# Up projection of an MLP: GpSimd instead of VectorE forms four sums of each unit's rectified blocks

## What is computed

```python
x = x + mixed @ w_out[l]
h = _rms_norm(x, norm_mlp_g[l])
x = x + jnp.square(jax.nn.relu(h @ w_up[l])) @ w_down[l]
return _rms_norm(x, norm_final_g)
```

## Time and profile before

| | before |
|---|---|
| median of 3 runs | 1518.6 us |
| the profiled execution | 1519.8 us |
| its span in the profile | 1518.0 us |
| TensorE busy in the span | 98% |
| VectorE busy | 72% |
| ScalarE busy | 52% |
| GpSimd busy | 1%, 28 instructions |
| mean granted TensorE clock | 0.996 |

### The profile page before, as it was taken

The page is one execution under the profiler, slowest core; times in us unless marked ns, Lnnn a source line. Parts: engine busy times, 40 slices in busy tenths (PEclk is TensorE's granted clock), DMA queues, the critical chain, the costliest instruction groups (busy, mean ns, idle before and its releaser), DMA issues.

```text
span 1518.0 us, 20760 instructions
## 1 busy us (share of the span) xinstructions
PE 1492.6 (98%) x7307; PEld 1239.0 (82%) x7307; DVE 1088.4 (72%) x1743; ACT 792.8 (52%) x1439; POOL 16.2 (1%) x28
## 2 busy tenths in 40 slices
PE   7999999999999999999999999999999899999998
PEld 6888888887888888888888888888888678888887
DVE  5787777756686778543765686667667798888886
ACT  6577766665677775444234553333334444444442
POOL 0000000000000200000000000000000000000000
PEclk9999999999999999999999999999999999999999
DMA  5221111114222014334545434444445864444402
GB/s 194 71 70 29 43 56 43 29 45 98 74 70 71 15 43 125 98 104 148 182 134 141 139 98 164 155 153 152 153 153 166 300 240 153 152 153 153 153 28 111
DMA packets 171061, 176.78 MB, mean 116 GB/s; under 512 B 9576, under 2 KB 129736, under 8 KB 170576
## 3 DMA queue, kind: packets, MB, share of 16 engines
q1 hardware_dynamic: 170960, 175.46, 36.4%
HBM read 129.08 MB, written 46.35 MB: 116 GB/s over the span
## 4 chain that ended last, share of the span: by engine, by line
PE 89%; DVE 5%; ACT 2%; issue 2%; DMA 1%; SPq 0%; DVEq 0%; ACTq 0%
PE ps L1547 39%; PE ps L1206 20%; PE ps L1407 8%; PE ps L1151 4%; PE ps L1438 4%; PE ps L1282 3%; PE ps L1249 3%; PE ps L1261 3%; PE ps L1348 1%; PE ps L1175 1%; PE ps L1140 1%; DVE keep L2410 1%; DVE keep L2305 1%; DVE ps L2283 1%; PE ps L1295 0%
## 5 line engine op out<-in xcount | busy, mean ns | idle before, releaser
L1206 PE MATMUL ps<-hspl,wsp 128*128 128x512 f32 x1536 | 419.6, 407 | 0.4 <-ACT tmp L1646 0.4
L1206 PEld LDWEIGHTS ps<-hspl,wsp 128*128 128x128 f32 x1536 | 265.8, 189 | 43.5 <-ACT tmp L1646 0.6
L1547 PE MATMUL ps<-dn_b,a_hi 128*128 128x512 f32 x896 | 278.5, 392 | 5.0 <-DVE keep L2410 3.6
L1547 PEld LDWEIGHTS ps<-dn_b,a_hi 128*128 128x128 f32 x896 | 169.0, 189 | 42.4 <-issue 7.4
L1547 PE MATMUL ps<-dn_b,a_lo 128*128 128x512 f32 x448 | 175.3, 391 | 0.0
L2410 DVE TENSOR_TENSOR keep<-keep,ps 128x512 f32<-128x512 f32 (+1 forms) x144 | 102.1, 713 | 59.1 <-PE ps L1547 39.3
L1547 PE MATMUL ps<-up_b,a_hi 128*128 128x512 f32 x384 | 118.4, 390 | 0.5 <-DVE up_b L2410 0.5
L2022 ACT ACTIVATE keep<-keep 128x512 f32<-128x512 f32 x64 | 40.5, 633 | 126.3 <-DVE keep L2717 41.9
L1547 PEld LDWEIGHTS ps<-dn_b,a_lo 128*128 128x128 f32 x448 | 84.8, 189 | 17.9
L2579 DVE TENSOR_TENSOR a_lo<-a_raw,a_hi 128x1024 fp32r<-128x1024 f32 (+1 forms) x66 | 81.3, 1234 | 9.5 <-ACT a_hi L1988 9.4
L1998 ACT COPY ps<-ps 128x512 f32<-128x512 f32 x46 | 26.3, 571 | 113.8 <-PE ps L1547 111.4
(11 more groups left out here) (229 smaller groups left out, 2803.6 us busy)
## 6 DMA issues: line engine op xcount, KB each, us to landing
hidden<-keep SPq DMA_DIRECT2D x112, 256.0 KB, 2.2
dn_raw<-hidden SPq DMA_DIRECT2D x56, 512.0 KB, 5.9
raw<-in_w_in SPq DMA_DIRECT2D x35, 512.0 KB, 3.8
a_raw<-in_w_up SPq DMA_DIRECT2D x36, 256.0 KB, 3.1
sgl<-sg SPq DMA_DIRECT2D x8, 1024.0 KB, 5.0
a_raw<-in_w_down SPq DMA_DIRECT2D x32, 256.0 KB, 3.0
spare<-in_w_down SPq DMA_DIRECT2D x32, 256.0 KB, 4.1
spare<-in_w_up SPq DMA_DIRECT2D x28, 256.0 KB, 3.2
```

Of the source, the lines that this page charges most:

```text
L1206: ins = pe.matmul(psp(u, g), wsp[c % 2][:, wp, k * P:(k + 1) * P], hspl[:, mp, k, cols], start=(n == 0), stop=(n == 23), skip_group_check= ...
L1547: ins = pe.matmul(o, a_part(n, j, wp, k), b_block(n, j, mp, k), start=(first and k == 0 and m == 0), stop=(k == ks - 1 and m == 2), skip_g ...
```

## The change

VectorE's loop no longer calls `t_sums(n - 2)`, for n = 2 to 15, which are the sums of units 0 to 13. GpSimd gets a loop over these 14 units with the same four operations, operands and semaphore counts. It stands between GpSimd's earlier work (L1121, done at 530 us) and its last (L1126, after 1500 us). The sums of units 14 and 15 stay with VectorE. No other wait and no DMA is changed.

```diff
@@ block.gpsimd @@
+            for q in range(UP - 2):
+                pool.wait_ge(u22_ok, q + 1)
+                pool.wait_ge(u12_ok, q + 1)
+                after(pool, t3_out, 16 * q)
+                pool.tensor_tensor(t3, u22[q % 2], u12, ALU.subtract).then_inc(t_ok, 1)
+                pool.wait_ge(u11_ok, q + 1)
+                after(pool, t2_out, 16 * q)
+                pool.wait_ge(t_ok, 4 * q + 1)
+                pool.tensor_tensor(t2, t3, u11[q % 2], ALU.add).then_inc(t_ok, 1)
+                pool.tensor_tensor(u12, u12, u11[q % 2], ALU.subtract).then_inc(t_ok, 1)
+                pool.wait_ge(u21_ok, q + 1)
+                after(pool, t4_out, 16 * q)
+                pool.wait_ge(t_ok, 4 * q + 2)
+                pool.tensor_tensor(t4, u21, t2, ALU.subtract).then_inc(t_ok, 1)
@@ block.vector, loop over n @@
                 if n >= 2:
                     up_r12(n - 2)
-                    t_sums(n - 2)
                 up_r21(n - 1)
```

## The result

The changed kernel takes 1543.3 us (median of 4 runs, 1542.9 to 1544.1), against 1517.9 us for the kernel before on the same chip: 25.4 us more, a ratio of 1.0165 (95% interval 1.0153 to 1.0178). Forecast were 26.6 us more. The profiled execution took 1544.1 us, its span is 1542.3.

The account below looks back on a forecast made before the run. TensorE, 98% busy, was taken to bound the kernel. Fourteen units at 2.74 us less 11.3 us of slack gave 27.1, less 0.48 us at TensorE 26.6 us late: 1545 us, range 1533 to 1555 (0.63).

Parts of the forecast that it names:

- What bounds, and no gain: Up stage, 896.0 to 1173.2 us: TensorE busy throughout, so taking work off VectorE gains nothing there.
- Price of the chain: Four sums on GpSimd: 5.37 us against VectorE's 2.72, with a later start +2.74 us per unit.
- The ring: Unit round through VectorE, ScalarE and DMA queue: 17.97 us grows to 20.71, exceeding TensorE's 19.04 per block.
- the slack of before: VectorE's wait at L2703 for ScalarE's copy L2018: 11.3 us over thirteen blocks, subtracted from the price.
- The cover of 0.36 us by the second ring: From L2717 over TensorE's P1 and copy L2018: VectorE released at R + 7.15, arriving at R + 7.51.
- Start of block 16: TensorE starts the down stage 26.6 us late, after its 0.48 us margin at that boundary.
- Behind block 16: Down stage: nothing new; the following stalls, 1.27 and 2.76 us, move along.
- 1, a slower GpSimd: GpSimd slower in the sums than in its eight additions: up to +44 us, 1555 to 1563; chance 0.12.
- 2, the clock: TensorE's granted clock falls after waits, 2.2 us each: +15 every second block, +30 all, 1560 to 1575; chance 0.14.
- 3, the slack covers it all: Chain of sums stays under 3.6 us, 0.9 us a sum, so no loss: 1518.6 us; chance 0.04.
- 4: The ring breaks somewhere, only part of 1.7 us per block is paid: 1522 to 1530 us; chance 0.06.
- What the profile would show: GpSimd 75 us busier, L2717 waiting in 14 blocks, TensorE waiting 1.5 to 2 us at P1, L2703's wait gone.

Follow-up runs that it names:

- e_bufv_load: The kernel before with a second u21 buffer and the a12 load issued ahead of the stores, all sums on VectorE: 1517.5 us, ratio 1.0000.
- e_buf_load: The changed kernel with a second u21 buffer and the a12 load issued ahead of the stores: 1517.1 us, ratio 0.9991.
- e_load: The changed kernel with the a12 load issued right behind P2, ahead of the stores of the sums and u21: 1536.6 us, ratio 1.0116.
- e_buf: The changed kernel with a second u21 buffer alone, the a12 load left behind the stores: 1537.3 us, ratio 1.0128.
- e_five: The changed kernel with a fifth same-size GpSimd operation between third and fourth sum in each of 14 units: 1563.9 us, ratio 1.0313.
- e_all_load: The kernel with two u21 buffers, the a12 load ahead of the stores and all 16 units' sums on GpSimd: 1518.0 us, ratio 0.9998.

## Why the prediction was right, point by point

**What bounds, and no gain.** Right. e_bufv_load and e_buf_load show that the stage is TensorE's as long as the rings are shorter than 19.04 us.

**Price of the chain.** Forecast +2.74 us a unit, measured 5.38 - 2.86 = 2.52 and 0.05 more at the start, 2.57. The terms: start after the square 0.14 us, not 0.18; spacing of the sums 1.25, not 1.275; GpSimd's wait for itself 0.17, not 0.24. The rows were the right ones, each a little too dear; these terms make up the 0.17 us, with 0.01 at the hand-over. The spacing from start to start was the better measure: the recorded durations of 1.29 would give 0.04 us more a sum.

**The ring.** Forecast 20.71 us, measured 20.35 to 20.52 in the nine usual blocks, 20.44 on average. Fourteen prices less the slack of before are 14 x 2.57 - 11.3 = 24.7 us; L2732 of unit 14 starts at 1197.82 against 1171.89, 25.9 us late, of which 0.45 were there before the stage. The 0.8 us that remain are a balance of several: one wait for the copy of P7 (1.2 us, below) and three late loads that were longer than the three of before (1.0 us together), against usual blocks 0.10 us shorter than the 17.97 + 2.57 = 20.54 of the sum.

**The cover of 0.36 us by the second ring.** Right in place, smaller in size: 20.27 us in e_load against 20.44 with the load in the ring, 0.17 us. For this reason one cut alone brings little back: e_load 6.7 us, more than half of it from the late loads that it hides, and e_buf 6.0; both together bring back all 25.4.

**Start of block 16.** Forecast 26.6 us late, measured 25.0 in the stage, 25.5 with what was there before it; the whole 25.4. The price was too high by 14 x 0.17 = 2.4 us, and the 0.8 us above stand against it. That the forecast of the time is off by only 1.2 us is thus partly luck: neither the low clock nor longer late loads were in the sum.

**Behind block 16.** Forecast: moves along unchanged. It did: TensorE's waits of 0.34, 0.95 and 2.75 us stand there again, where they were 0.34, 0.93 and 2.76. Not foreseen is that the half clock behind the last was shorter: the granted clock is 0.79 in 8 us of after and 0.59 in the same 8 us of before, and the lateness falls from 25.5 us to the 24.3 by which the spans differ. Nothing in the change explains this difference. Windows of after, then of before:

```profile
1177.00:1180.50 3.50, 3.50 (x10) 2.68 (x10) 1.05 (x2) 0.70 (x2) 0.00 (x0) 0.53 0.69 225
...
1221.80:1229.80 8.00, 5.90 (x19) 4.75 (x20) 6.20 (x8) 3.77 (x5) 0.00 (x0) 0.79 0.87 284
```

```profile
1196.20:1204.20 8.00, 5.87 (x14) 4.64 (x15) 5.31 (x7) 3.74 (x5) 0.00 (x0) 0.59 0.87 278
```

**The rivals.** 1, a slower GpSimd, did not come: VectorE stood still and nothing disturbed the sums. e_buf_load shows what the disturbance is where they meet. 2, the clock, came once: after the wait of 2.37 us before 1175.83, which follows a late load, the granted clock was 0.53 from 1177.0 to 1180.5 (the first of the rows above) and the copy of P7 was 1.2 us late. It never fell behind the ten waits of 0.98 to 1.24 us, but not behind the longest of the stage either, 2.65 us before 990.06. So the mechanism was real, the price of 2.2 us for each fall was too high (1.2 here, 0.8 to 1.4 in e_five), and which wait it follows stays open; e_five brings it six times in the stage, in every second block from 970 us on, as the rival had it. 3, the slack covers it all, needed a chain of 3.6 us and got 1008.17 + 1.29 - 1004.21 = 5.25. 4 is out: both ties are where they were read.

**What the profile would show.** GpSimd's 71 us, the groups of four, L2732's fourteen waits and the lost wait for the copy came as said. TensorE's waits were forecast as 1.5 to 2 us and are 0.98 to 1.24 us in ten of the fourteen blocks; the others, 1.73 and 2.65 and 2.37 us, follow late loads, and 1.92 the low clock.

## What to carry to other kernels

Close the ring before pricing a change of engine: follow one unit through all in-order queues, DMA issue included, until it comes back to itself, and compare the sum with the period of the engine that bounds. Where it closes on the period with a visible wait, that wait is the slack, and everything above it is paid in every round. Look for the next ring too, for it says what a repair will bring: here each cut alone gave back about a quarter, both gave everything. And an operation moved off a busy engine earns nothing if that engine waits for its result, or if it was not the late one. No run here gained by the move; to be of use it would need another buffer, a place where the engine is late, and work to do there meanwhile that does not read SBUF with two inputs.

## What the runs showed of the hardware

Where GpSimd and a VectorE instruction with two SBUF inputs meet, the one that starts later lasts longer, by a little less than the time for which they overlap, and the one that was there first does not. In e_buf_load VectorE's subtraction starts at 1000.30, 0.46 us before the first sum ends, and lasts 0.32 us more than its 1.22; the second sum starts at 1000.93, 0.91 us before the subtraction ends, and lasts 0.77 us more than its 1.29. The first sum, which was there first, keeps its 1.30. The seven meetings in the rows of e_all_load, from 1184.71 to 1191.75, do the same: each later one grows by 0.12 to 0.15 us less than the overlap, for example the fourth sum by 1.52 us with 1.64 of overlap. Two instructions look as if they lengthened each other only because each is the later one of a different pair. The Trainium skill (SBUF — State Buffer, Who interferes with whom) says that a VectorE instruction with two SBUF inputs contends with a GpSimd instruction that reads SBUF, and that the order of issue decides who blocks; the trace agrees. So the cost of putting GpSimd beside such work is close to the overlap, whichever engine pays it.

Late loads go with code loads. In the kernel before the a12 load released VectorE after 2.96 to 3.11 us in ten blocks and after 3.70, 3.75 and 3.92 us in three, and in just these three a packet of the instruction queue q8 was under way. In the changed kernel it was 3.60, 4.25 and 4.57 us with such a packet, and one load of 3.10 us had one without harm. The DMA queues while the load of 969.00 us ran, in the changed kernel (kind: packets, MB, share of 16 engines):

```profile
q8 instruction: 1, 0.02, 1.8%
```

That the packet causes the delay is a reading of this coincidence; no run took it away. In the kernel before, the slack hid these late loads; in the changed kernel each lengthened its block, to 21.97, 21.01 and 21.65 us.

The granted clock fell to half after waits of TensorE of 2.08 to 2.92 us in e_five of 2.37 and 2.75 us in after and of 2.76 us in the kernel before, but it stayed at 1.00 behind waits of 2.15 and 2.30 us in e_five, of 2.65 us in after, and of 2.76 us in e_load. The rows are of the last two: first TensorE and the window behind its wait in after, then e_load's, here in the 8 us that answer to those of before and after. The length of one wait alone does not tell it.

```profile
990.06 0.70 PE L1562 MATMUL ps<-up_b,a_hi 128*128 128x512 f32 x2 [2.65 <-DVE keep L2732]
```

```profile
990.06:996.06 6.00, 6.00 (x26) 4.96 (x27) 3.68 (x6) 3.01 (x5) 0.00 (x0) 1.00 0.66 211
...
1214.70:1222.70 8.00, 5.92 (x26) 4.96 (x27) 6.81 (x9) 3.65 (x5) 0.00 (x0) 1.00 0.84 277
```

What such a fall costs shows behind block 16. In e_load this block starts 1191.52 - 1173.20 = 18.3 us later than in the kernel before, but the span is only 1532.6 - 1518.0 = 14.6 us longer. An estimate from the clocks (0.59 against 1.00 over 8 us) gives 3.3 of the 3.7 us between. Differences of a few microseconds between medians of four executions are to be read with that in mind.
